# First loads in a new order, and stick-breaking steps set between projections

## The chip, the core and the metric

One NeuronCore of a Trainium2 chip runs the whole program. The metric is the device time of one launch in microseconds, lower is better. TensorE (PE) does matmuls, VectorE (DVE) and ScalarE (ACT) the elementwise work, GpSimd (POOL) and SyncE (SP) here mostly issue DMAs. Each engine runs its own instruction queue in order, and the engines meet only through semaphores.

## What is computed

Four transformer-like layers over 512 tokens of width 1024, in float32. Two parts of it matter here. Every layer begins with an RMS norm whose output is scaled and shifted by a modulation computed from a condition vector:

```
cond = silu(c)
mod  = cond @ ada_w[layer] + ada_b[layer]            # 6 x 1024 values
h    = rms_norm(x, mix_norm[layer]) * (1 + sc1) + sh1
```

Layer 0 then projects h to several outputs. The first, iq and ik, get rotary embeddings (tables of cosines and sines made from the positions) and feed a top-k choice of keys. The queries and keys of its attention, dq and dk, get another pair of tables.

Layer 1 has a pooling branch and stick-breaking attention with four heads of width 128:

```
u, sq, sk, sv = split(h @ w_in)                      # 512 columns each
o_pool = scale * ((trailing mean of u over 2, 4, 8, 16 tokens) - u) @ pool_w
q, k   = rms_norm(sq), rms_norm(sk)                  # per head
z      = q k^T / sqrt(128)
log_1m = where(s < t, log_sigmoid(-z), 0)
after  = reverse cumulative sum of log_1m over keys, less log_1m
w      = where(s < t, exp(log_sigmoid(z) + after), 0)
y      = concat(o_pool, w v) @ w_out
```

## The kernel before

Activations lie with features on partitions: a tile is 128 features x 512 tokens. `T(i)` is scratch tile i, `X(k)` the residual stream, `H(k)` the normed input. Weights come in chunks of 512 KB through a ring of four slots that SP fills, each when the slot's last use is over. Two PSUM rings of four banks each hold results: `proj` for projections, `mix` for everything else. The order in which banks are taken is written out in `mixing_keys` and `projection_keys`, and a bank is taken again only when its earlier user has emptied it. There is no planner: the order on each engine is the order of the program text.

Most projections are split: ScalarE rounds a weight chunk to a short float (`round_chunk`, `weight_hi`), VectorE computes the rest (`rest_chunk`, `weight_lo`), each in a ring of two, and TensorE does three matmuls per 128 rows: hi x hi, hi x lo, lo x hi. A feature tile of such a projection (`split_feature_tile`, L778) is 24 matmuls of 128x512; so is one of the four quarters of a token projection (`split_token_tiles`, L792). `first_pair` does tiles 0 and 1 of the first projection behind a norm together.

**The start.** ScalarE issues the loads of the sixteen modulation rows that the first norm needs (L1388), 512 KB each, four rows per semaphore. SP loads two tables of constants (`others`, `vectors`), the square matrices (`squares`, 768 KB) and x (2 MB), waits for the first eight rows, and then loads weights. GpSimd loads c, positions and small weights, waits for the last four rows and reloads the ring for the next modulation rows. ScalarE then computes silu(c). VectorE multiplies and reduces each row (L2002); before rows 4 and 8 it makes two rotation tables each (`rotation_table`, L1851 to L1855), whose sines ScalarE takes. ScalarE squares x for norm(0) behind the sines. VectorE sums six of the eight squares behind the sixteen rows (`sum_up`), TensorE sums over partitions (`row_sums`, L839), ScalarE takes the root, VectorE the reciprocal (L1899), TensorE spreads it (`spread_rows`, L848), VectorE scales the tiles (L1910) and ScalarE shifts them. The first projection (iq, L702) begins with the first shifted tile. Behind tile t of iq, TensorE does the swap of tile t-1 (L853) for its rotation, which needs a square matrix and ScalarE's copy of the projection.

**The stick-breaking stage.** The order is norm(2), cu (the pooled u), sq, sk, sv, then the pooling maps, then the heads. For sq and sk ScalarE copies and squares a tile (`head_stat`), TensorE sums it (L1008), ScalarE takes a root, VectorE a reciprocal and the product; the split of the next weight chunk stands between these in both queues. Then head h goes through: scores (TensorE, L1020, four banks), copies, exp and ln (ScalarE, `z_ready`), softplus and masks (VectorE, `sp_ready`), sums over keys (TensorE, L1027 and L1029), subtraction (VectorE), exp of the weights (ScalarE, `w_ready`), product with V (TensorE, L1041), rounding and rest for the output projection cdo. The loop over h overlaps neighbouring heads: scores of h, sums of h-1, product with V of h-2. `pair_step` then does tiles 0 and 1 of cdo for one of its eight inputs, and the other six tiles follow (L756).

Of the kernel before, what the change touches and what calls it, by code (L numbers as in the profile page):

```python
# [21 lines left out]
I32 = mybir.dt.int32  # L22
# [22 lines left out]
SPLIT_RING = 2  # L45
FIRST_ROWS = (0, 2, 4, 6, 8, 14, 16, 18, 20, 22, 24, 26, 28, 34, 36, 38)
# [100 lines left out]
for _name, _n in VECTORS:  # L147
# [10 lines left out]
    ("cu", "feat", 4, 8), ("sq", "feat", 4, 8), ("sk", "feat", 4, 8), ("sv", "tok", 4, 8), ("cdo", "loop", 8, 8),  # L158
# [14 lines left out]
SPLIT = ("abo", "up0", "dn0", "cu", "sq", "sk", "sv", "cdo", "up1", "dn1", "mqk", "mv", "mo", "mout", "up2", "dn2", "cout", "up3", "dn3", "rk", "rq", "rv", "fv", "ru", "rg", "br", "ro", "upr", "dnr")  # L173
# [38 lines left out]
def mixing_keys():  # L212
# [43 lines left out]
    return k  # L256

# [27 lines left out]
class Chip:  # L285


    def __init__(self, nc, ctx, dram):
# [37 lines left out]
        with ExitStack() as mlstm:  # L326
# [15 lines left out]
        self.first_rows = [sem(f"first_rows{i}") for i in range(4)]  # L342
        self.ada_landed = [sem(f"ada_landed{i}") for i in range(ADA_RING)]
        self.sem = {n: sem(n) for n in (
            "x_loaded", "c_loaded", "constants", "setup", "late", "pool_loaded", "dft_loaded", "cond_loaded", "ctx_loaded", "late_tables", "act_chain", "dve_chain",
# [65 lines left out]
    def cdo_hi(self, k):  # L411
        return self.R(k if k < 4 else 14 + k)

# [136 lines left out]
def sync_program(nc, sp, c):  # L550

    d, s = c.dram, c.sem
    for dst, src in ((c.other, d["others"]), (c.vec, d["vectors"]), (c.sq_const, d["squares"])):
        sp.dma_start(dst[:, :], src).then_inc(s["constants"], 16)
    sp.dma_start(c.x[:, :].rearrange("p (k t) -> p k t", k=KD), d["x"].rearrange("(k p) t -> p k t", p=P)).then_inc(s["x_loaded"], 16)

    proj = c.proj
    sp.wait_ge(c.first_rows[1], 16 * 4)
# [4 lines left out]
    for stage in STAGES:  # L563
# [59 lines left out]
def gpsimd_program(nc, pool, c):  # L623
# [23 lines left out]
    pool.wait_ge(c.first_rows[3], 16 * 4)  # L647
# [34 lines left out]
def tensor_program(nc, pe, c):  # L682
# [142 lines left out]
    def norm(r):  # L825

        n = stat_count(r)
        pe.wait_ge(s["sq_summed"], 6 * (n + 1))
        row_sums(r, T(SQ0), False)
        pe.wait_ge(s["sq_ready"], 8 * (n + 1))  # L830
        row_sums(r, T(SQ0 + KD - 1), True)
        pe.wait_ge(s["rstd_ready"], r + 1)
        spread_rows(r, 1)

    def row_sums(r, squares, last_half):

        bank = (mix.bank(("ss", r)) if last_half else open_bank(mix, ("ss", r)))[0:4, 0:P]
        for j in range(NB):
            last = mm(bank, c.const("pick")[:, 4 * j:4 * j + 4], squares[:, j * P:(j + 1) * P], start=not last_half and j == 0,  # L839
                      stop=last_half and j == NB - 1)  # L840
        if last_half:
            last.then_inc(mix.full_sem, 1)
# [19 lines left out]
    pe.wait_ge(s["constants"], 16 * 3)  # L862
    pe.wait_ge(s["setup"], 16 * 4)
    norm(0)
    for t in range(6):
# [5 lines left out]
        if t == 4:  # L871
            for n in range(NB):
# [126 lines left out]
    norm(2)  # L999
    first_pair("cu", 2, c.H_lo)  # L1000
    for t in range(2, 4):
        split_feature_tile("cu", t, c.H_hi, c.H_lo)
    for t in range(9):
        if t < 8:
            split_feature_tile("sq" if t < 4 else "sk", t % 4, c.H_hi, c.H_lo)
        if t >= 1:
            pe.wait_ge(*proj.emptied(("sq" if t <= 4 else "sk", (t - 1) % 4)))
            mm(open_bank(mix, ("stat_s", t - 1)), c.square("ones"), T(20 + (t - 1) % 2), start=True, stop=True).then_inc(mix.full_sem, 1)  # L1008
    split_token_tiles("sv", 0, c.H_hi, c.H_lo)
    for g in range(4):  # L1010
# [4 lines left out]
    pe.wait_ge(s["head_normed"], 8 + 4 + 8)  # L1015
    pe.wait_ge(*proj.emptied(("sv", 3)))
    for h in range(6):
        if h < 4:
            for j in range(NB):
                mm(open_bank(mix, ("z", h, j))[:, 0:S - P * j], T(14 + h)[:, j * P:(j + 1) * P], T(10 + h)[:, j * P:S],  # L1020
                   start=True, stop=True).then_inc(mix.full_sem, 1)
        if 1 <= h <= 4:
            pe.wait_ge(s["sp_ready"], h)
            sp = T(34 + 3 * ((h - 1) % 2), 3)
            for j in range(NB):
                bank = open_bank(mix, ("cum", h - 1, j))
                last = mm(bank[:, 0:S - P * j], c.square("later"), sp[:, TRI[j]:TRI[j + 1]], start=True, stop=j == NB - 1, skip_group_check=True)  # L1027
                for i in range(j + 1, NB):
                    last = mm(bank[:, P * (i - j):S - P * j], c.square("ones"), sp[:, TRI[i]:TRI[i + 1]], start=False,  # L1029
                              stop=i == NB - 1, skip_group_check=True)  # L1030
                last.then_inc(mix.full_sem, 1)
        if h == 5:
            for k in range(6):
                pe.wait_ge(*mix.emptied(("pool", k) if k < 4 else ("sb", k - 4)))
# [1738 lines left out]
```

## Time and profile before

| what | value |
|---|---|
| median of 3 runs | 3664.53 us (3664.01 to 3669.24) |
| the profiled execution | 3674.72 us |
| its span | 3673.1 us |
| busy: PE, PEld, DVE, ACT, POOL | 92%, 68%, 56%, 32%, 3% |
| mean granted TensorE clock | 0.957 of 2.4 GHz |

Busy time counts instructions that work, not waits. PEld are TensorE's weight loads, which overlap its matmuls. A clock of 1.00 is 2.4 GHz, 0.5 is 1.2 GHz. In a timeline, "[7.93 <-DVE scratch L1847]" means that the engine had been idle for 7.93 us and was released by that instruction. Nearly all VectorE tensor_tensor operations have the line of a helper, L1847, and ScalarE's have L1276.

### The profile page before, as it was taken

The numbers are of one execution on the slowest core, as the hardware profiler recorded it, in microseconds if no ns is written. First come the engines' busy times: TensorE is split into PE (matmuls) and PEld (weight loads), VectorE is DVE, ScalarE is ACT, GpSimd is POOL, SyncE is SP. The second block draws the span as 40 slices with busy tenths as digits, with TensorE's granted clock in tenths as the row PEclk, the third lists the DMA queues.
The fourth block names the chain that finished last, engine by engine and source line by source line (L and its number), as shares of the span: only waits on it lengthen the run. The fifth ranks groups of instructions, "written<-read, shape, count | busy, mean of one in ns | idle before, by whom it ended". The sixth has DMA issues, their size and how long they took to land. (4 is left out here: it accounts for less than half of the span.)

```text
span 3673.1 us, 37941 instructions
## 1 busy us (share of the span) xinstructions
PE 3367.4 (92%) x13358; PEld 2494.2 (68%) x13358; DVE 2059.4 (56%) x2808; ACT 1173.0 (32%) x1503; POOL 111.0 (3%) x204
## 2 busy tenths in 40 slices
PE   2998689999979999998999999799999999979997
PEld 1444468887647888666788864478887657758886
DVE  5757456544647884546666359766634553345523
ACT  2211333323443221444445210244423242232221
POOL 0000000000000000000000030000000000000000
PEclk9998699999989999999999999899999999989999
DMA  5332035643204563212223321123333222222232
GB/s 201 121 123 91 12 97 189 194 134 119 67 29 137 189 196 101 81 52 64 80 92 97 98 62 52 40 80 97 96 95 121 73 69 75 92 63 92 95 99 69
DMA packets 100417, 361.01 MB, mean 98 GB/s; under 512 B 11152, under 2 KB 11168, under 8 KB 100064
## 3 DMA queue, kind: packets, MB, share of 16 engines
q1 hardware_dynamic: 77936, 276.08, 23.9%
q0 software_dynamic: 20080, 75.27, 6.4%
q10 hardware_dynamic: 2304, 8.39, 0.6%
q8 instruction: 58, 0.95, 0.1%
q14 instruction: 39, 0.32, 0.0%
HBM read 357.59 MB, written 2.10 MB: 98 GB/s over the span
## 5 line engine op out<-in xcount | busy, mean ns | idle before, releaser
L1847 DVE TENSOR_TENSOR weight_lo<-weight_ring,weight_hi 128x1024 fp32r<-128x1024 f32 (+1 forms) x462 | 557.3, 1207 | 988.8 <-ACT weight_hi L1276 982.9
L1276 ACT ACTIVATE weight_hi<-weight_ring 128x1024 fp32r<-128x1024 f32 (+1 forms) x462 | 482.3, 1045 | 1515.0 <-PE proj_banks L756 1066.5
L756 PE MATMUL proj_banks<-h_lo,weight_hi 128*128 128x512 f32 x1776 | 694.5, 391 | 0.0
L756 PE MATMUL proj_banks<-h_hi,weight_hi 128*128 128x512 f32 x1344 | 525.7, 391 | 13.7 <-DVE weight_lo L1847 13.7
L756 PE MATMUL proj_banks<-h_hi,weight_lo 128*128 128x512 f32 x1344 | 525.8, 391 | 0.0
L756 PEld LDWEIGHTS proj_banks<-h_lo,weight_hi 128*128 128x128 f32 x1776 | 335.7, 189 | 70.1
L756 PEld LDWEIGHTS proj_banks<-h_hi,weight_hi 128*128 128x128 f32 x1344 | 254.0, 189 | 68.1 <-issue 15.3
L756 PE MATMUL proj_banks<-mid_lo,weight_hi 128*128 128x512 f32 x768 | 299.2, 390 | 0.0
L756 PEld LDWEIGHTS proj_banks<-h_hi,weight_lo 128*128 128x128 f32 x1344 | 253.5, 189 | 52.9
L756 PE MATMUL proj_banks<-mid_hi,weight_hi 128*128 128x512 f32 x704 | 273.9, 389 | 0.0
L756 PE MATMUL proj_banks<-mid_hi,weight_lo 128*128 128x512 f32 x704 | 273.9, 389 | 0.0
L702 PE MATMUL proj_banks<-h_tiles,weight_ring 128*128 128x512 f32 x592 | 260.9, 599 | 1.8 <-ACT h_tiles L1276 1.8
L1276 ACT ACT_TABLE_LOAD x133 | 170.6, 1283 | 259.0 <-PE proj_banks L756 109.8
L702 PEld LDWEIGHTS proj_banks<-h_tiles,weight_ring 128*128 128x128 f32 x592 | 113.5, 192 | 145.2 <-issue 143.2
L756 PE MATMUL proj_banks<-relu_hi,weight_hi 128*128 128x512 f32 x468 | 183.0, 391 | 7.6 <-DVE weight_lo L1847 7.6
L1847 DVE TENSOR_TENSOR scratch<-scratch 128x512 f32<-128x512 f32 (+5 forms) x226 | 160.1, 708 | 45.2 <-ACT small L1276 32.0
L1276 ACT ACTIVATE scratch<-proj_banks 128x512 f32<-128x512 f32 (+1 forms) x186 | 104.9, 574 | 229.9 <-PE proj_banks L702 127.5
L1855 DVE SCALAR_TENSOR_TENSOR scratch<-proj_banks,vectors,scratch 128x511 f32<-128x511 f32 (+3 forms) x208 | 155.2, 746 | 27.9 <-ACT scratch L1276 14.4
L756 PEld LDWEIGHTS proj_banks<-mid_lo,weight_hi 128*128 128x128 f32 x768 | 144.1, 188 | 30.2 <-issue 0.2
L1855 DVE SCALAR_TENSOR_TENSOR scratch<-scratch,vectors 128x512 f32<-128x512 f32 x212 | 159.4, 752 | 7.5
L756 PE MATMUL proj_banks<-relu_hi,weight_lo 128*128 128x512 f32 x404 | 157.8, 390 | 0.0
L756 PEld LDWEIGHTS proj_banks<-mid_hi,weight_hi 128*128 128x128 f32 x704 | 132.1, 188 | 27.5
(342 smaller groups left out, 4871.5 us busy)
## 6 DMA issues: line engine op xcount, KB each, us to landing
weight_ring<-in_w_up SPq DMA_DIRECT2D x176, 512.0 KB, 3.6
ada_ring<-in_ada POOLq DMA_DIRECT2D x96, 512.0 KB, 3.9
weight_ring<-in_w_dn SPq DMA_DIRECT2D x64, 512.0 KB, 3.5
weight_ring<-in_w_br SPq DMA_DIRECT2D x32, 512.0 KB, 3.6
weight_ring<-in_w_upr SPq DMA_DIRECT2D x32, 512.0 KB, 3.5
weight_ring<-in_w_dnr SPq DMA_DIRECT2D x32, 512.0 KB, 3.5
scratch<-in_ada POOLq DMA_DIRECT2D x24, 512.0 KB, 4.4
weight_ring<-in_w_dn SPq DMA_DIRECT2D x32, 384.0 KB, 3.1
```

The source lines that it names most:

```text
L702: last = mm(bank[:, 0:n], c.slot(chunk)[:, i * P:(i + 1) * P], rhs(k), start=k == 0, stop=k == sum(per) - 1)
L756: last = mm(proj.banks[:, u % RING, :], stationary(split0 + n)[:, w], moving(k), start=k + m == 0, stop=k == kt - 1 and m == 2)
L1276: return nc.scalar.activation(out, in_, func, **kw)
L1847: return v.tensor_tensor(out, a, b, op)
L1855: return v.scalar_tensor_tensor(out=out, in0=a, scalar=x, in1=b, op0=op0, op1=op1)
```

## The change

At the start: the row loads are shared, eight on ScalarE's queue and eight on SP's behind x; each row has its own semaphore. SP's wait for rows is gone; `squares` is loaded behind the second weight chunk. The rotation tables leave the row loop: the pair for i comes behind norm(0), the pair for q behind the top-k. norm(0) has no sums on VectorE: TensorE sums each squared tile as it comes, and the reciprocal is done before the last two rows. TensorE waits for `squares` before the first projection.

In layer 1: cu moves behind sv. Nine slots follow the four quarters of sv and the four tiles of cu, and slot numbers say what stands in each: scores, sums, product with V, pooling maps. `cdo_lo` gets tiles of its own and the weights of odd heads another place in scratch.

```diff
+ACT_ROWS = 8
+TRIG = (12, 13, 10, 11)
-    k += [("stat_s", t) for t in range(8)] + [("pool", g) for g in range(4)]
-    for h in range(6):
-        k += [("z", h, j) for j in range(NB)] if h < 4 else []
-        k += [("cum", h - 1, j) for j in range(NB)] if 1 <= h <= 4 else []
-        k += [("sb", h - 2)] if h >= 2 else []
+    k += [("stat_s", t) for t in range(8)] + [("z", 0, j) for j in range(NB)]
+    for slot in range(SB_SLOTS):
+        k += [("z", SB_SCORES[slot], j) for j in range(NB)] if slot in SB_SCORES else []
+        k += [("cum", SB_SUMS[slot], j) for j in range(NB)] if slot in SB_SUMS else []
+        k += [("sb", SB_VALUES[slot])] if slot in SB_VALUES else []
+        k += [("pool", g) for g in SB_POOLS.get(slot, ())]
+    k += [("sb", 3)]
+SB_SLOTS = 9
+SB_SCORES = {1: 1, 3: 2, 5: 3}
+SB_SUMS = {1: 0, 3: 1, 5: 2, 7: 3}
+SB_VALUES = {4: 0, 5: 1, 7: 2}
+SB_POOLS = {6: (0,), 7: (1,), 8: (2, 3)}
@@ sync_program
-    for dst, src in ((c.other, d["others"]), (c.vec, d["vectors"]), (c.sq_const, d["squares"])):
+    for dst, src in ((c.other, d["others"]), (c.vec, d["vectors"])):
+    for r in range(ACT_ROWS, len(FIRST_ROWS)):
+        sp.dma_start(c.T(FIRST_ROWS[r], 2), d["ada"][r]).then_inc(c.first_rows[r], 16)
-    sp.wait_ge(c.first_rows[1], 16 * 4)
+            if first + n == 1:
+                sp.dma_start(c.sq_const[:, :], d["squares"]).then_inc(s["squares_in"], 16)
@@ gpsimd_program
-    pool.wait_ge(c.first_rows[3], 16 * 4)
+    pool.wait_ge(c.first_rows[ACT_ROWS - 1], 16)
+    pool.wait_ge(c.first_rows[-1], 16)
@@ tensor_program
+        if r == 0:
+            for k in range(KD):
+                pe.wait_ge(s["sq_ready"], k + 1)
+                row_sums(r, T(SQ0 + k), k == 0, k == KD - 1)
...
     norm(0)
+    pe.wait_ge(s["squares_in"], 16)
...
+    norm(2)
+    first_pair("sq", 2, c.H_lo)
+    for t in range(1, 9):
+        if 2 <= t < 8:
+            split_feature_tile("sq" if t < 4 else "sk", t % 4, c.H_hi, c.H_lo)
+        pe.wait_ge(*proj.emptied(("sq" if t <= 4 else "sk", (t - 1) % 4)))
+        mm(open_bank(mix, ("stat_s", t - 1)), ...)
+    stick_scores(0)
+    split_token_tiles("sv", 0, c.H_hi, c.H_lo, between=stick_between)
+    for t in range(4):
+        split_feature_tile("cu", t, c.H_hi, c.H_lo)
+        stick_between(4 + t)
+    stick_between(8)
+    for k in (0, 1, 4, 5):
...
+        pair_step("cdo", k, c.cdo_hi, c.cdo_lo)
+    stick_values(3)
+    for k in (2, 3, 6, 7):
...
+        pair_step("cdo", k, c.cdo_hi, c.cdo_lo)
@@ scalar_program
-    for r, at in enumerate(FIRST_ROWS):
-        act.dma_start(T(at, 2), c.dram["ada"][r]).then_inc(c.first_rows[r // 4], 16)
+    for r in range(ACT_ROWS):
+        act.dma_start(T(FIRST_ROWS[r], 2), c.dram["ada"][r]).then_inc(c.first_rows[r], 16)
...
+    norm(0)
+    for n in range(2):
+        trig(n)
...
+    softplus_parts(0)
+    for slot in range(SB_SLOTS):
+        if slot < 8:
+            round_s(8 + slot + SPLIT_RING)
+        if slot == 3:
+            for t in range(4):
+                copy_out(proj, ("sv", t), T(24 + t))
+        if 4 <= slot < 8:
+            copy_out(proj, ("cu", slot - 4), T(slot - 4))
+        if slot in SB_SCORES:
+            softplus_parts(SB_SCORES[slot])
+        if slot in SB_SUMS:
+            stick_weights(SB_SUMS[slot])
+        if slot in SB_VALUES:
+            stick_hi(SB_VALUES[slot])
+        for g in SB_POOLS.get(slot, ()):
...
+    stick_hi(3)
@@ vector_program
     for r, at in enumerate(FIRST_ROWS):
-        dve.wait_ge(c.first_rows[r // 4], 16 * 4)
-        if r in (4, 8):
...
+        if r == len(FIRST_ROWS) - 2:
+            inverse_root(0)
+        dve.wait_ge(c.first_rows[r], 16)
...
     norm(0)
+    for n in range(2):
+        rotation_table(n)
+    dve.wait_ge(s["trig_ready"], 2)
...
+    softplus(0)
+    for slot in range(SB_SLOTS):
+        if slot < 8:
+            rest_s(8 + slot + SPLIT_RING)
+        if slot in SB_SCORES:
+            softplus(SB_SCORES[slot])
+        if slot in SB_SUMS:
+            stick_left(SB_SUMS[slot])
+        if slot in SB_VALUES:
+            sb_rest(SB_VALUES[slot])
+        for g in SB_POOLS.get(slot, ()):
+            pool_rest(g)
+        if 4 <= slot < 8:
+            pooled(slot - 4)
```

`stick_scores`, `stick_sums`, `stick_values`, `pool_map`, `softplus_parts`, `stick_weights`, `softplus`, `stick_left` hold the bodies of the old loop over h. The second pair of tables is made behind the top-k on VectorE; ScalarE takes its sines between its copies of gk and gv.

## Rows read from the trace of the kernel before

**Rows 1.** TensorE waits, whole run: group, releaser, us in total, times, longest
```profile
PE mix_banks L839 <- DVE scratch L1847: 88.5, 3, 64.4
...
PE mix_banks L1041 <- DVE scratch L1847: 16.1, 3, 7.9
```

**Rows 2.** Stretches: length, busy us of PE/PEld/DVE/ACT/POOL, PEclk, DMA share, GB/s
```profile
889.90:1121.70 231.80, 192.95 (x744) 143.11 (x744) 127.66 (x162) 97.21 (x133) 0.00 (x0) 0.91 0.17 52
...
1000.00:1073.00 73.00, 43.49 (x137) 26.78 (x136) 35.08 (x64) 43.32 (x60) 0.00 (x0) 0.79 0.04 11
...
1046.89:1053.60 6.71, 6.71 (x30) 4.58 (x28) 0.69 (x1) 6.16 (x12) 0.00 (x0) 1.00 0.01 2
...
921.53:926.57 5.04, 5.04 (x24) 4.18 (x23) 4.69 (x12) 1.91 (x3) 0.00 (x0) 1.00 0.32 104
...
155.00:332.00 177.00, 177.00 (x409) 78.28 (x410) 123.68 (x221) 37.83 (x60) 6.33 (x12) 0.99 0.32 104
```

**Rows 3.** The same view of ten microseconds near the start
```profile
30.00:40.00 10.00, 0.00 (x0) 0.00 (x0) 9.52 (x18) 1.26 (x2) 0.00 (x0) 1.00 1.03 410
```

**Rows 4.** DMA issues in the first 10 us: tile, queue, count, size, us to landing
```profile
x_tiles<-in_x SPq DMA_DIRECT2D x1, 2048.0 KB, 27.4
...
cond<-in_c POOLq DMA_DIRECT2D x1, 512.0 KB, 9.3
```

**Rows 5.** Timeline, start: start us, length, engine, line, tiles, count, idle
```profile
20.12 1.28 ACT L1276 ACT_TABLE_LOAD   x1 [20.12 <-issue]
...
22.50 1.22 DVE L2002 CUSTOM_DVE_ANT_0 scratch<-scratch,cond 128x1024 f32<-128x1024 f32 x1 [22.50 <-ACT cond L1276]
...
27.57 0.43 DVE L1999 CAST scratch<-scratch 128x512 f32<-128x512 int32 x1
...
36.13 1.23 DVE L2002 CUSTOM_DVE_ANT_0 scratch<-scratch,cond 128x1024 f32<-128x1024 f32 x1
...
42.57 1.62 POOL L640 DMA_DIRECT2D ada_ring<-in_ada  x3 [38.41 <-DMA scratch<-in_ada]
...
50.03 4.60 ACT L1276 ACTIVATE scratch<-x_tiles 128x512 f32<-128x512 f32 x7
...
59.85 4.33 DVE L1847 TENSOR_TENSOR scratch<-scratch 128x512 f32<-128x512 f32 x6
...
68.56 0.94 DVE L1899 RECIPROCAL scratch<-scratch 4x128 f32<-4x128 f32 x1 [4.38 <-ACT scratch L1276]
...
71.75 6.23 DVE L1855 SCALAR_TENSOR_TENSOR h_tiles<-x_tiles,gain,mix_banks 128x512 f32<-128x512 f32 x8 [2.25 <-PE mix_banks L848]
...
73.46 15.66 PE L702 MATMUL proj_banks<-h_tiles,weight_ring 128*128 128x512 f32 x32 [1.83 <-ACT h_tiles L1276]
...
88.96 1.02 PE L853 MATMUL mix_banks<-scratch,squares 128*128 128x512 f32 x2
...
89.82 7.03 PE L702 MATMUL proj_banks<-h_tiles,weight_ring 128*128 128x512 f32 x16
```

**Rows 6.** Timeline of VectorE at the gate arithmetic
```profile
271.14 5.78 DVE L1847 TENSOR_TENSOR scratch<-scratch 128x512 f32<-128x512 f32 x8 [32.05 <-ACT small L1276]
```

**Rows 7.** Timeline of TensorE: sq and sk projections, stick-breaking, output projection
```profile
945.44 0.47 PE L778 MATMUL proj_banks<-h_hi,weight_hi 128*128 128x512 f32 x1 [0.46 <-DVE weight_lo L1847]
...
952.62 0.47 PE L778 MATMUL proj_banks<-h_hi,weight_hi 128*128 128x512 f32 x1 [0.60 <-DVE weight_lo L1847]
...
1043.08 3.97 PE L1041 MATMUL mix_banks<-scratch 128*128 128x512 f32 x8 [7.93 <-DVE scratch L1847]
...
1088.89 0.47 PE L756 MATMUL proj_banks<-relu_hi,weight_hi 128*128 128x512 f32 x1 [1.88 <-DVE weight_lo L1847]
```

**Rows 8.** Timelines of ScalarE and VectorE in the stick-breaking heads
```profile
1002.00 3.16 ACT L1276 ACTIVATE scratch<-mix_banks 128x512 f32<-128x512 f32 x8 [0.17 <-PE mix_banks L1020]
...
1010.52 1.49 DVE L1855 SCALAR_TENSOR_TENSOR scratch<-scratch 128x1280 f32<-128x1280 f32 x1 [7.84 <-ACT scratch L1276]
...
1024.63 2.05 DVE L1847 TENSOR_TENSOR scratch<-scratch,mix_banks 128x512 f32<-128x512 f32 x4
```

More of the change, by code:

```diff
@@ L1014, in tensor_program @@
         mm(open_bank(mix, ("pool", g)), c.pool_w[:, g * P:(g + 1) * P], T(6 + g), start=True, stop=True).then_inc(mix.full_sem, 1)
[L1015 to L1034, printed above, removed]
-                pair_step("cdo", k, c.cdo_hi, c.H_lo)
-        if h >= 2:
-            pe.wait_ge(s["w_ready"], h - 1)
-            w = T(40 + 3 * (h % 2), 3)
-            bank = open_bank(mix, ("sb", h - 2))
-            for j in range(NB):
-                last = mm(bank[:, P * j:S], T(24 + j)[:, (h - 2) * P:(h - 1) * P], w[:, TRI[j]:TRI[j + 1]], start=j == 0,
-                          stop=j == NB - 1, skip_group_check=True)
-            last.then_inc(mix.full_sem, 1)
@@ L1422, in scalar_program @@
         copy_out(proj, ("gk", t), T(28 + t))
+    for n in range(2, 4):
+        trig(n)
     for t in range(4):
@@ new lines, in softplus_parts @@
+    def softplus_parts(h):
+        z, l = T(28 + 3 * (h % 2), 3), T(34 + 3 * (h % 2), 3)
+        for j in range(NB):
+            act.wait_ge(*mix.filled(("z", h, j)))
+            bank = mix.bank(("z", h, j))[:, 0:S - P * j]
+            f(z[:, TRI[j]:TRI[j + 1]], bank, ACT.Copy, scale=P ** -0.5)
+            st.last(f(l[:, TRI[j]:TRI[j + 1]], bank, ACT.Abs, scale=P ** -0.5), mix.emptied(("z", h, j)))
+        l = l[:, 0:TRI[4]]
+        st.link(f(l, l, ACT.Exp, scale=-1.0))
+        st.done(f(l, l, ACT.Ln, bias=c.const("one")), s["z_ready"])
@@ L1890, in sum_up, with inverse_root @@
             st.done(tt(H(0), H(0), H(k), ALU.add), s["final_summed"])
+    def inverse_root(r):
+        dve.wait_ge(*mix.emptied(("ss", r)))
+        st.done(v.reciprocal(T(RSTD)[0:4, P:2 * P], T(RSTD)[0:4, 0:P]), s["rstd_ready"])
     def norm(r):
-        if r not in NORM_AFTER:
+        if r not in NORM_AFTER and r > 0:
             for k in range(1, KD - 1):
@@ L2042, in vector_program @@
         st.link(ts(T(16 + b)[:, 0:width], score, -2e38, ALU.is_gt, NEG, ALU.mult))
+    for n in range(2, 4):
+        rotation_table(n)
+    dve.wait_ge(s["trig_ready"], 4)
+    st.link(ts(T(11), T(11), c.const("sign_q"), ALU.mult))
     ada_rows(15, 8)
@@ L2233, in vector_program, with pool_rest @@
                 s["head_normed"])
-    for n in range(12 + SPLIT_RING, 16):
-        rest_s(n)
-    for g in range(4):
+    def pool_rest(g):
         dve.wait_ge(s["pool_hi"], g + 1)
-        st.last(stt(c.H_lo(g), mix.bank(("pool", g)), c.v("pool_scale", g), c.cdo_hi(g).bitcast(F32), ALU.mult, ALU.subtract), mix.emptied(("pool", g)))
+        st.last(stt(c.cdo_lo(g), mix.bank(("pool", g)), c.v("pool_scale", g), c.cdo_hi(g).bitcast(F32), ALU.mult, ALU.subtract), mix.emptied(("pool", g)))
     def sb_rest(h):
@@ new lines, in sb_rest, with softplus @@
+        st.last(tt(c.cdo_lo(4 + h), mix.bank(("sb", h)), c.cdo_hi(4 + h).bitcast(F32), ALU.subtract), mix.emptied(("sb", h)))
+    def softplus(h):
+        z, sp = T(28 + 3 * (h % 2), 3)[:, 0:TRI[4]], T(34 + 3 * (h % 2), 3)[:, 0:TRI[4]]
+        dve.wait_ge(s["z_ready"], h + 1)
+        st.link(stt(sp, z, 0.0, sp, ALU.max, ALU.add))
+        for j in range(NB - 1):
+            w = slice(TRI[j], TRI[j] + P)
+            st.link(tt(sp[:, w], sp[:, w], c.square("strict"), ALU.mult))
+        w = slice(TRI[3], TRI[3] + P)
+        st.done(tt(sp[:, w], sp[:, w], c.square("strict"), ALU.mult), s["sp_ready"])
+        st.link(tt(z, z, sp, ALU.subtract))
+        for j in range(NB):
+            w = slice(TRI[j], TRI[j] + P)
+            st.link(tt(z[:, w], z[:, w], c.square("strict_neg"), ALU.add))
@@ new lines, in stick_left @@
+    def stick_left(h):
+        z = T(28 + 3 * (h % 2), 3)
+        for j in range(NB):
+            key = ("cum", h, j)
+            dve.wait_ge(*mix.filled(key))
+            w = z[:, TRI[j]:TRI[j + 1]]
+            st.last(tt(w, w, mix.bank(key)[:, 0:S - P * j], ALU.subtract), mix.emptied(key))
+    softplus(0)
+    for slot in range(SB_SLOTS):
+        if slot < 8:
+            rest_s(8 + slot + SPLIT_RING)
+        if slot in SB_SCORES:
+            softplus(SB_SCORES[slot])
+        if slot in SB_SUMS:
+            stick_left(SB_SUMS[slot])
+        if slot in SB_VALUES:
+            sb_rest(SB_VALUES[slot])
+        for g in SB_POOLS.get(slot, ()):
+            pool_rest(g)
+        if 4 <= slot < 8:
+            pooled(slot - 4)
```

206 lines of the change are left out of this document (87 added, 119 removed).

## The prediction

> **What bounds the kernel now.** I read the shares by engine first: TensorE is busy 92% of the span, so time can only be won where TensorE waits or runs at its lower clock. The list of TensorE's waits then names the places. The longest by far is 64.4 us before the first row-sum matmul of norm(0), and the heads' product with V (L1041) waits 16.1 us in three times [rows 1]. These are the two places that the change touches.
>
> The start: VectorE begins when silu(c) is there, at 22.50, because ScalarE first issues all sixteen modulation rows and is free only at 20.12. Then it alternates between row reductions and rotation tables, sums the squares of x, and the first projection starts at 73.46 [rows 5]. The DMA engines are full then, at 410 GB/s [rows 3].
>
> The stick-breaking stage runs from 889.9 to 1121.7. Its middle, 1000 to 1073, has 43.49 us of TensorE in 73, at a granted clock of 0.79; the stage as a whole has 0.91 [rows 2]. In this stretch each head waits in turn for ScalarE (copies, exp, ln), VectorE (softplus, masks, subtraction) and ScalarE again (exp), with no projection left to fill the gaps. Between 155 and 332 TensorE is busy without a pause [rows 2], so a shift at the start passes through there undiminished.
>
> **The start, step by step.** Before the last modulation row lands, these must come: sixteen rows of 512 KB, x, the two constant tables, c, positions and small weights, 12.48 MB by their shapes. Before the change the squares (0.79 MB) and four weight chunks (2.10 MB) moved in the same time, 15.36 MB in all, and GpSimd, which waits for the last rows, went on at 42.57 [rows 5]. 2.88 MB at 410 GB/s [rows 3] are 7.0 us, so the last row lands at 35.5.
>
> VectorE reduces a row in 1.27 us (four of them from 22.50 to 27.57, [rows 5]), and a row takes 0.524 MB / 410 GB/s = 1.28 us to land. ScalarE issues eight rows instead of sixteen, which took it until 20.12: about 10. c landed at 1.4 + 9.3 = 10.7 [rows 4], a table load and silu take 2.4 more, so VectorE starts near 13 instead of 22.5. Fourteen rows at 1.27 are then done at 31, ahead of the loads, the tables being gone from the loop. (Had it started at 22.5, sixteen rows would end at 42.8.) The reciprocal of norm(0), 0.94 [rows 5], now stands before the last two rows and delays them by about 1.0: row 13 lands at 33.0 and is done at 34.2, the reciprocal at 35.2, the rows at 36.5 and 37.8. Bias and gain take 0.4, and from the first scaled tile to the first projection are 1.71 (71.75 to 73.46): 39.9. The six sums (4.33) and the chain from sums to spread root (64.4 to 71.75) have left this path. They are replaced by eight row sums on TensorE, which is idle then. x has to be there in time. It was issued at 2.3 and landed 27.4 later, at 29.7 [rows 4], behind the squares; their 0.79 MB at the full rate are 1.9 us, at a third of it 5.8, so it now lands between 24 and 27.8. Seven squares of x take 4.60 [rows 5], a table load 1.28, the eighth, the row sums and the root about 1.9: 32 to 35.6, against a turn of the reciprocal at 34.2. The late end costs 1.4 us, which the next wait covers.
>
> The change adds a wait: TensorE waits for the squares before the first projection, and they now stand behind two weight chunks on SP's queue. Unshared they land when 14.32 of the 15.36 MB are through, 42.57 - 1.04/0.41 = 40.0. GpSimd's four rows start when the last first row has landed; if they take half the rate from 35.5 on, 1.84 MB need 9.0 us: 44.5. I take the middle, 42.2. All of TensorE's program is queued behind that wait. But a late start is partly made good: from the first matmul to the first swap were 15.50 us (73.46 to 88.96), paced by the scaling of tiles at 6.23 for eight, and at full pace two projections take 2 x 6.87 = 13.7 (a tile's 7.03 less the overlap, [rows 5]). So the first swap is at 55.9 instead of 88.96: 33.0 us earlier. With squares at 40.0 it would be 33.5, at 44.5 30.8.
>
> Two tables (the i pair) now follow the scaling on VectorE: 44.5 + 8.6 (27.57 to 36.13, with the cast, [rows 5]) = 53.1, the sine 0.63 and the sign 0.5 make 54.2. ScalarE's copy of the first projection is queued behind these sines and TensorE's swap behind the copy; both are ready 1 to 2 us before 55.9. Without that cover each late microsecond would cost one. The q pair (8.1 and a sign of 0.5) comes after the top-k, where VectorE has 32.05 us of idle time waiting for ScalarE's exponentials [rows 6]: nothing, and 8.6 if that slack were gone. ScalarE's copies of gv stand behind these sines, and the copies' input is later than they. SP's waits on rows vanish; GpSimd's reload of rows starts earlier by the same shift. The head is worth 33.0.
>
> **The stick-breaking stage.** The stage now runs sq, sk, sv, cu, with pieces of the heads after chosen quarters of sv and tiles of cu. Matmul work does not change. The terms: a tile or quarter of a projection 5.47 (six output tiles in 1121.7 - 1088.89, [rows 2, 7]); scores and sums of one head 6.7 at full clock [rows 2]; product with V 2.1; ScalarE from scores to z_ready 8.5 (1002.00 to 1010.52); VectorE's softplus and masks 5.6, its subtraction 2.05 [rows 8]; exp of the weights with its table load 2.6; the widest pooling 5.0 (the stretch from 921.53 to 926.57, [rows 2]).
>
> The sq and sk tiles run at a period of 7.18 (945.44 to 952.62, [rows 7]) because VectorE's reciprocal and split stand between them. This stays. But it is six tiles after the first pair and not eight, the first pair being sq itself. So TensorE is through with statistics at 950.7. From there its work to the end of the paired output steps is 26.8 (scores, sums) + 21.9 (sv) + 21.9 (cu) + 8.3 (V) + 3.4 (pool) + 10.9 (eight pair steps) = 93.2.
>
> I wrote all three engines' queues down in their new order and worked them forward with these durations. Three gaps stay on TensorE:
> First, the sums of head 1. VectorE does softplus(1) from 973.4, then the subtraction of head 0, until 981.1. ScalarE waits for it, then exp, two weight roundings, four copies of sv, and only then the copies of the scores that free the banks: 989.4. TensorE was done with the scores at 983.9: 5.5 us.
> Second, the product with V of head 1. It needs the bank of head 2's first sum, which VectorE frees after z_ready(3) at 1018.1, softplus 5.6 and the first subtraction 0.7: 1024.5. TensorE was free at 1016.6: 7.9 us.
> Third, the pooling of group 3, which VectorE reaches last: 5.8 us.
> With two of 0.5 this is 20.2 us. Each large gap is followed by matmuls at the lower clock: the product with V after a 7.93 gap took 3.97 [rows 7] and not 2.1, so 2 us each, 6 together. 950.7 + 93.2 + 20.2 + 6.0 = 1070.1. The same hand run of the old order ends at 1085.3 where the trace has 1087.0 (1088.89 - 1.88, [rows 7]), so I add 1.7: 1071.8, 15.2 earlier. The 1.88 before the third output tile stays, as does the rest of the stage. Bounds of this term: if every slot costs a gap of the longest kind, there are five slots with sums or V in them, 5 x 7.9 = 40 instead of 20, and the gain is -5; if the gaps and their slow clock halve, 28.
>
> **Sum.** 33.0 + 15.2 = 48.2. The profiled execution took 3674.72 us (span 3673.1), so it would take 3626.5. The runs shown have a median of 3664.53, 10.2 below the profiled one; the same saving gives 3616.3.
>
> **The rivals.** Changes of less than 0.2% (7 us) can't be told from none here.
> (a) The forecast: 40 to 56 us saved, 3608 to 3624. Chance 0.70.
> (b) x comes last. VectorE's queue is in order and the reciprocal stands before rows 14 and 15. If x landed only with the last row at 35.5, its squares, the root (7.8) and the reciprocal (0.9) would end at 44.2, the two rows at 46.8, bias and scaling put the first matmul at 48.9 and the swap at 64.4: the head saves 24.6, all 39.8, 3624.7. For it speaks that x is the largest transfer and landed 27.4 us after its issue; against it, that more stood before it then [rows 4]. Chance 0.09. The Trainium skill (DMA: Bandwidth & Descriptors, queues, rings and completion order) says that a DMA engine takes turns between the queues packet by packet, so a queue with shorter packets gets fewer bytes; x's rows are half as long as a modulation row's. Its slow landing agrees.
> (c) The stage's gaps only move. The roundings of weights stand behind softplus in both queues, and if a projection also waits for its split in each of the five slots, the stage saves 0: 33 in all, 3631.5. For it: VectorE and ScalarE are in-order and nearly every slot has a handshake. Against: in the run by hand each split was ready before its tile. Chance 0.12.
> (d) Slower: TensorE stays at the lower clock. If after the first gap every further one came before the clock had recovered, all 99 us of work from 950.7 to the pair steps would run at half speed, 99 more, of which 20 fill the gaps: 79 lost against 48 saved, 3695. It turns slower from 68 of the 99 us at half speed. For it: 0.79 between 1000 and 1073. Against it: right behind the slow product with V the clock was 1.00, from 1046.89 to 1053.60 [rows 2], and the projections between make blocks of 5 us and more. The Trainium skill (TensorE: Matmul & The Clock Gate, loop structure matters more than you think) has the rule that long waits between bursts put the clock at half; the trace agrees with the row of 3.97. Chance 0.02.
> (e) The gaps are half as long as computed: 13 us more, 3603. Chance 0.07.
>
> **The numbers.** The likeliest is 3616.3, its own range 3608 to 3624. From 3604 to 3630 hold (a), (b) and about half of (c) and (e), 0.85 to 0.9 if each is right, and I leave the rest for errors of mine. Faster by over 0.2% are (a), (b), (c) and (e): 0.97, with 0.01 for no change and 0.02 for (d).
>
> **What would show it.** First projection matmul at 40 to 44, first swap near 56, GpSimd's first reload near 35.5: the head. If the matmul is later and its releaser is the DMA of the squares, the queue term was off; if VectorE idles before its reciprocal, it was x. VectorE's long idle at the gate arithmetic should be near 23 instead of 32. In the stage: waits of about 5 to 8 us before the sums of head 1, the product with V of head 1 and the pooling of group 3, and 216.6 us from the first pair to the end of the output projection. Waits of L778 or L792 on weight_lo between slots would speak for (c), a granted clock below 0.8 from there for (d). The prediction fails if the stage is no shorter or if the last row does not land before 40.

## The result, and the profile after

The changed kernel takes 3626.61 us (median; 3613.92 to 3628.97) against 3666.89 of the kernel before on the same chip: a ratio of 0.989, 95% interval 0.9873 to 0.9907, so 34 to 47 us faster. The forecast was 3616.3. A second measurement, on another occasion, gave 3621.46 against 3664.46: 0.9882 (0.9867 to 0.9897), 38 to 49 us. The saving forecast, 48.2, lies just past the upper end of the first and just inside that of the second. The median is 10.3 above the forecast: outside its likeliest range, 3608 to 3624, and inside the 3604 to 3630 that was given with it.

The profiled execution took 3627.46 (span 3625.8), where 3626.5 was forecast for it. That agreement flatters: two errors meet in it, as the experiments show.

Timelines of the changed kernel's start (start us, length, engine, line, operation, count, idle before it and what ended it), from all four engines, to be held against [rows 5]:
```profile
0.87 4.74 ACTq L1439 DMA_DIRECT2D scratch<-in_ada  x8
...
2.27 19.38 SPq L577 DMA_DIRECT2D scratch<-in_ada  x8
...
10.31 1.06 ACT L1327 ACTIVATE cond<-cond 128x1024 f32<-128x1024 f32 x1 [3.39 <-DMA cond<-in_c]
...
25.30 4.60 ACT L1327 ACTIVATE scratch<-x_tiles 128x512 f32<-128x512 f32 x7 [13.94 <-DMA x_tiles<-in_x]
...
26.03 8.93 PE L868 MATMUL mix_banks<-scratch,others 128*4 128x128 f32 x64 [26.03 <-ACT scratch L1327]
...
35.52 0.94 DVE L1963 RECIPROCAL scratch<-scratch 4x128 f32<-4x128 f32 x1 [1.29 <-ACT scratch L1327]
...
36.00 1.62 POOL L663 DMA_DIRECT2D ada_ring<-in_ada  x3 [31.83 <-DMA scratch<-in_ada]
...
39.44 6.23 DVE L1923 SCALAR_TENSOR_TENSOR h_tiles<-x_tiles,gain,mix_banks 128x512 f32<-128x512 f32 x8
...
41.15 1.19 PE L726 MATMUL proj_banks<-h_tiles,weight_ring 128*128 128x512 f32 x1 [3.48 <-ACT h_tiles L1327]
```
Silu no longer waits for ScalarE's queue but for c. GpSimd's reload, which waits for the last rows, comes at 36.00 (forecast 35.5), the scaling of the tiles at 39.44 instead of 71.75. The first projection is released by ScalarE's tile at 41.15, not by the DMA of the squares, whose load was issued at 23.7 and landed 16.1 later: the added wait costs nothing, and the 42.2 forecast for it was too late by 1.0. The first swap is at 57.76, against 88.96 and a forecast of 55.9.

TensorE's waits in the stick-breaking stage of the changed kernel, from 920 to 1050 (group, releaser, us in total, times, longest):
```profile
PE mix_banks L1056 <- DVE scratch L1915: 8.1, 2, 7.9
PE mix_banks L1042 <- ACT scratch L1327: 6.3, 2, 5.6
PE mix_banks L1065 <- DVE scratch L1915: 5.9, 1, 5.9
```
These are the three gaps that the prediction computed as 7.9 (product with V of head 1), 5.5 (sums of head 1) and 5.8 (pooling of group 3). The stage in the timeline of TensorE: its first pair, the first matmuls behind the three gaps, and the third output tile:
```profile
864.16 0.80 PE L740 MATMUL proj_banks<-h_hi,weight_hi 128*128 128x512 f32 x1 [1.65 <-ACT h_hi L1327]
...
964.03 2.05 PE L1042 MATMUL mix_banks<-scratch,squares 128*128 128x512 f32 x2 [5.60 <-ACT scratch L1327]
...
999.60 3.84 PE L1056 MATMUL mix_banks<-scratch 128*128 128x512 f32 x8 [7.85 <-DVE scratch L1915]
...
1029.32 2.07 PE L1065 MATMUL mix_banks<-scratch 128*128 128x512 f32 x2 [5.86 <-DVE scratch L1915]
...
1047.32 0.70 PE L780 MATMUL proj_banks<-relu_hi,weight_hi 128*128 128x512 f32 x2 [1.89 <-DVE weight_lo L1915]
```
The matmuls behind each gap run slowly, as forecast: 3.84 for the product with V that takes 2.39 elsewhere. The third output tile starts at 1047.32, 183.2 after the first pair. In the kernel before the first pair is at
```profile
890.15 0.79 PE L716 MATMUL proj_banks<-h_hi,weight_hi 128*128 128x512 f32 x1 [1.66 <-ACT h_hi L1276]
```
and the third output tile at 1088.89 [rows 7], 198.7 later. 15.6 saved, 15.2 forecast.

### The profile page after: what moved, and what is told of

It is laid out like the page before. It is cut to its first block and busy times, and to the rows that moved or that the text cites. A ratio compares the mean times of both kernels' runs of the same rounds, so it can differ in the third digit from the quotient of the medians.

```text
span 3625.8 us, 38035 instructions
## 1 busy us (share of the span) xinstructions
PE 3365.5 (93%) x13406; PEld 2495.2 (69%) x13406; DVE 2055.4 (57%) x2802; ACT 1174.1 (32%) x1504; POOL 111.0 (3%) x204
## 5 line engine op out<-in xcount | busy, mean ns | idle before, releaser
L780 PE MATMUL proj_banks<-h_lo,weight_hi 128*128 128x512 f32 x1728 | 676.2, 391 | 0.0
L780 PEld LDWEIGHTS proj_banks<-h_lo,weight_hi 128*128 128x128 f32 x1728 | 326.7, 189 | 67.8
L780 PE MATMUL proj_banks<-relu_hi,weight_hi 128*128 128x512 f32 x516 | 194.5, 392 | 7.6 <-DVE weight_lo L1915 7.6
L1915 DVE TENSOR_TENSOR scratch<-scratch 128x512 f32<-128x512 f32 (+6 forms) x220 | 155.9, 709 | 37.5 <-ACT small L1327 24.4
```

What stands on the lines that cost most here:

```text
L780: last = mm(proj.banks[:, u % RING, :], stationary(split0 + n)[:, w], moving(k), start=k + m == 0, stop=k == kt - 1 and m == 2)
L1915: return v.tensor_tensor(out, a, b, op)
```

## The experiments

Ratios are to the kernel before, run on the same chip. Times of single runs without a ratio are not compared; those runs were made for their profiles. Where a kernel has lines added, its line numbers are up to six higher than those of the changed kernel.

**The two halves.** *start_only* is the kernel before with the start of the change, *stage_only* with the new order of the stage; *after_again* is the changed kernel beside them. The edit of *stage_only*, cut to its core:
```diff
+SB_SCORES = {1: 1, 3: 2, 5: 3}
+SB_SUMS = {1: 0, 3: 1, 5: 2, 7: 3}
+SB_VALUES = {4: 0, 5: 1, 7: 2}
...
+    split_token_tiles("sv", 0, c.H_hi, c.H_lo, between=stick_between)
```
and of *start_only*:
```diff
+    for r in range(ACT_ROWS):
+        act.dma_start(T(FIRST_ROWS[r], 2), c.dram["ada"][r]).then_inc(c.first_rows[r], 16)
...
+        dve.wait_ge(c.first_rows[r], 16)
```


> The kernel before with the start of the change alone (rows, squares, tables, row sums); the stick-breaking stage is the old one. Theory A (the two parts are independent, each keeps what the traces show): first swap at 57.8 us, 31 earlier; of that 26 arrive at norm(1), and 26 to 31 at the end: timed ratio to before 0.992 to 0.993. Rival B (the shift is eaten later, by waits on weights or the reload of modulation rows, and the whole measured gain is the stage's): 0 to 15 us at the end, ratio 0.996 to 1.

> The kernel before with the new order of the stick-breaking stage alone; the start is the old one. Theory A: from the first pair of the stage to norm(3) 216 us instead of 231.6, and 15.2 to 15.6 us less at the end, ratio 0.9958. Rival B (the stage's gain shows up only because it starts at another phase of the granted clock): stage 225 or more, ratio 0.998 to 1.

> The changed kernel once more, beside its two halves on one chip. Theory A: the two halves add up, so the ratio is the product of theirs, 0.988 to 0.989, 41 to 46 us. Rival B (they overlap or disturb each other): less than the larger half plus 5 us.

Measured: *start_only* 3637.0, ratio 0.9923 (0.9909 to 0.9936), 23 to 33 us faster. *stage_only* 3654.68, ratio 0.9973 (0.9963 to 0.9983), 6 to 14 us faster. Their product is 0.9896, inside *after_again*'s interval. So both parts are real, and within these intervals nothing speaks against their adding up; some three quarters of the gain is the start. But *stage_only*'s own profile shows the full 15.6 in the stage, and its median gains 9.8. That is below what the profile promised, and its interval ends at 13.6.

**The profile of before, once more.**

> The kernel before, unchanged, profiled once more. Theory A (the profile shown of before had more of the lower clock in stretches that the change does not touch): first swap at 88.9 to 89.0 again, norm(1) at 503 to 507 instead of 509.0, the stage from norm(2) to norm(3) 237 to 238.5, span near 3663. Rival B (that profile is the typical one and the kernels made since gain outside the changed code): norm(1) at 509, span 3670 or more.

Its first row sum of norm(1), in the timeline of TensorE:
```profile
506.90 1.04 PE L839 MATMUL mix_banks<-scratch,others 128*4 128x128 f32 x8
```
The profile shown of before has this at 509.02, and *stage_only*, whose start is the old one, at 503.54. The same instructions on the same waits differ by 5.5 us there; at the end the two profiles of before are 9.5 apart (3674.72 and 3665.21). Theory A holds in kind: the profile shown is one of the longer executions. The norm(1) of *before_again* is at the late end of the range I gave, its span is 3663.5.

**Where the spread comes from.** The whole stage, norm(2) to norm(3), in windows (length, busy us of PE, PEld, DVE, ACT, POOL, granted clock, DMA share, GB/s). In the changed kernel:
```profile
857.19:1080.17 222.98, 190.72 (x769) 142.47 (x768) 133.16 (x167) 99.58 (x136) 0.00 (x0) 0.94 0.18 57
```
and in *warm_start* (below), whose stage has the same instructions:
```profile
846.57:1074.49 227.92, 195.30 (x770) 145.72 (x769) 133.21 (x167) 99.63 (x136) 0.00 (x0) 0.92 0.18 56
```
TensorE's idle time is 32.3 and 32.6. What differs is its busy time, by 4.6, at a granted clock of 0.92 instead of 0.94: VectorE and ScalarE work for the same time to 0.1. The stage took 222.98, 223.00 and 222.96 in *after*, *after_again* and *stage_only*, and 227.92, 227.94, 227.89 and 227.77 in *warm_start*, *rows_on_act*, *bytes_in_front* and *tables_in_loop*. The Trainium skill (TensorE: Matmul & The Clock Gate, What's actually happening) says that how many matmuls run before the clock rises varies from run to run; the two windows agree, and show a price of 5 us a stage.

The old stage took 238.5 in the profile shown of before, 237.4 in *before_again* and 237.3 in *start_only*. Four of seven profiles have the long form, so the new order is worth 14.3 to 15.6 in one form and 9.3 to 10.8 in the other, and *stage_only*'s 9.8 lies where a mixture of both would. The runs without a profile can't be sorted into the two, so that is an inference. Nor is chance told from the chip: the three profiles from chip 1 are long, the two from chip 3 short.

Stretches that no edit touches vary too: from the row sums at 2736.38 to the end the changed kernel took 889.4, *before_again* 889.2 and *start_only* 882.2, with TensorE busy for 829.9, 829.9 and 822.8 of it, so the ends of two profiles can differ by 7 us without any change.

**Two causes named for the start.** *rows_on_act* lets ScalarE issue all rows; *bytes_in_front* moves loads ahead of SyncE's rows:
```diff
-ACT_ROWS = 8
+ACT_ROWS = 16
...
+    sp.wait_ge(c.first_rows[8], 16)
```
```diff
+    sp.dma_start(c.sq_const[:, :], d["squares"]).then_inc(s["squares_in"], 16)
+    for n in range(4):
+        sp.dma_start(c.slot(n), d["w_iq"][n]).then_inc(c.landed[n % RING], 16)
     for r in range(ACT_ROWS, len(FIRST_ROWS)):
...
```


> The changed kernel, but ScalarE issues all sixteen rows (SyncE's queue waits for row 8 before its weights). Theory A (silu, and with it VectorE's first row, waits until ScalarE has issued its rows): silu ends near 22.5, VectorE is busy without a pause until 43.9, first projection at 46 instead of 41.2, first swap near 62.2, 4.5 later. Rival B (the landing of the rows sets the pace, VectorE follows): first projection within 1 us of 41.2.

> The changed kernel, but SyncE issues the squares and the first four weight chunks (2.88 MB) ahead of its eight rows. Theory A (the start is bound by bytes before the last row): last row 7.0 us later, first projection near 46.4 instead of 41.2, GpSimd's reload near 43. Rival B (VectorE's 1.28 us a row sets the end, the loads have slack): first projection within 1.5 us of 41.2.

The first projection matmul of *rows_on_act*, in the timeline:
```profile
45.28 3.75 PE L727 MATMUL proj_banks<-h_tiles,weight_ring 128*128 128x512 f32 x4 [2.85 <-ACT h_tiles L1328]
```
and timelines of *bytes_in_front*: a row of VectorE, GpSimd's reload, the first projection:
```profile
33.71 1.23 DVE L2072 CUSTOM_DVE_ANT_0 scratch<-scratch,cond 128x1024 f32<-128x1024 f32 x1 [7.80 <-DMA scratch<-in_ada]
...
43.05 1.62 POOL L665 DMA_DIRECT2D ada_ring<-in_ada  x3 [38.89 <-DMA scratch<-in_ada]
...
47.02 1.19 PE L728 MATMUL proj_banks<-h_tiles,weight_ring 128*128 128x512 f32 x1 [2.56 <-ACT h_tiles L1329]
```
Both as theory A has it. With the rows on ScalarE the first projection is 4.1 later (46 expected, 45.28 seen) and the first swap, at 62.04, 4.3. The Trainium skill (DMA: Bandwidth & Descriptors, Issuing engines are not separate DMA queues) says that issuing from several engines saves only sequencer time, usually small beside the transfer. Here sixteen issues held ScalarE until 20.12 [rows 5] and eight for 4.74, and in this place it decides when silu can run. With 2.88 MB in front VectorE waits 7.80 for one row and the reload moves from 36.00 to 43.05: 7.05, as 2.88 MB at 410 GB/s say. The start has two constraints that are nearly even; either alone holds it. A third is the row sums, for which the reciprocal waited 1.29 in the changed kernel and not at all in these two. But norm(1) came at 483.4 and 481.8 in these two, and at 478.9 to 484.6 in the five profiles with the changed kernel's start (*after*, *after_again*, *spread*, *left_first*, *values_later*): 4 to 6 us at the first swap were not to be seen there (below).

**The tables.** All four go back between the rows:
```diff
+        if r in (4, 8):
...
+            for n in (r // 2 - 2, r // 2 - 1):
+                rotation_table(n)
```


> The changed kernel with all four rotation tables back between the modulation rows on VectorE, two before row 4 and two before row 8. Theory A (the tables lengthen VectorE's chain, which has only some 5 us of idle time among the rows): VectorE busy from 11.4 to about 50, first projection near 51.6 instead of 41.2, first swap near 67, 9 later. Rival B (the landing of the rows hides the tables): first projection before 44.5.

```profile
48.19 2.07 PE L877 MATMUL mix_banks<-scratch,others 4*128 4x128 f32 x8 [12.28 <-DVE scratch L1963]
...
52.83 16.86 PE L726 MATMUL proj_banks<-h_tiles,weight_ring 128*128 128x512 f32 x32 [2.56 <-ACT h_tiles L1327]
```
In these rows of its TensorE timeline the spread of the root waits 12.28 for the reciprocal, and the first projection is 11.7 later than with the tables behind the scaling; the swap, at 69.53, 11.8. I expected 10.4 and 9. Of the three pieces undone this is the largest. The sums and the root with its reciprocal, which held VectorE's path from 59.85 to 71.75 [rows 5] and now lie beside the rows, were not put back by themselves.

**The clock of the first projections.** TensorE gets matmuls to do while it would be idle; their result is overwritten unread.
```diff
+    for r in range(6):
+        pe.wait_ge(c.first_rows[r], 16)
+        for _ in range(2):
+            mm(proj.bank(("iq", 0)), c.other[:, 0:P], c.other[:, 0:S], start=True, stop=True)
     norm(0)
+    for _ in range(2):
+        mm(proj.bank(("iq", 0)), c.other[:, 0:P], c.other[:, 0:S], start=True, stop=True)
```


> The changed kernel with 14 more matmuls on TensorE that nobody reads: two behind each of the first six modulation rows, two between the spread root and the first projection. Theory A (the start lost 2 us against the forecast because idle TensorE is granted 1.2 GHz): the row sums end near 33 instead of 35.0, the reciprocal does not wait (1.29 gone), the first projections run at the full clock from the start, first swap at 54.4 instead of 57.8, set then by the copy behind the second sine; 3 us less at the end. Rival B (VectorE's scaling of the tiles paces the first projection and the sines the swap, whatever the clock): the swap at 57 or later, nothing at the end.

The windows from the first projection matmul to the first swap, first of the changed kernel, then of *warm_start*:
```profile
41.15:57.76 16.61, 16.61 (x33) 7.21 (x34) 12.88 (x22) 8.05 (x11) 0.00 (x0) 0.83 0.42 164
```
```profile
41.57:56.17 14.60, 13.97 (x32) 5.96 (x32) 12.89 (x22) 8.06 (x12) 0.00 (x0) 1.00 0.47 178
```
At the full clock the two projections take 13.97 instead of 16.61; the forecast had 13.7. The tiles are scaled as fast as before (6.23 for eight), so it was the clock that paced the projections, as theory A says; of rival B the sines remain. The swap is then 1.6 earlier, no longer 3.4, because the copy behind the second sine ends last (0.64 of idle): the cover of 1 to 2 us that the prediction named is used up.

The other half of theory A, the row sums, was not put to the test by this edit. Stretches of 3 us show it by the number of matmul records in them (the x behind TensorE's busy time), two of the changed kernel and one of *warm_start*:
```profile
26.03:29.03 3.00, 3.00 (x15) 1.85 (x16) 2.38 (x3) 2.87 (x5) 0.00 (x0) 1.00 1.02 406
31.03:34.03 3.00, 3.00 (x30) 2.39 (x28) 2.92 (x5) 1.00 (x3) 0.00 (x0) 1.00 1.04 414
```
```profile
26.59:29.59 3.00, 3.00 (x15) 1.80 (x16) 2.34 (x3) 2.87 (x5) 0.00 (x0) 0.50 1.03 410
```
In the changed kernel the first 3 us hold 15 row-sum records and a later 3 us hold 30: half pace, then full pace. Its clock column says 1.00 for both, but its trace has no clock record before 29.7, and the view then shows 1.00. *warm_start* has a record there, 0.50 with the same 15, after TensorE had been idle for 3.61 between the last unread matmul and the row sums. So both run their first row sums at 1.2 GHz, in 8.93 and 8.79 us for all 64 records, and the reciprocal still waits 1.10. At full pace the row sums would end near 33, just behind the last square (32.08), and the reciprocal would not wait; that is an estimate from these rows, and no run tried it.

The same holds for the kernel before at its first projection, where the count goes from 4 to 8:
```profile
73.46:76.46 3.00, 3.00 (x4) 1.44 (x5) 2.86 (x5) 2.75 (x5) 0.00 (x0) 1.00 0.00 0
78.46:81.46 3.00, 3.00 (x8) 1.33 (x7) 0.64 (x2) 0.28 (x1) 0.00 (x0) 1.00 0.00 0
```
Timed, *warm_start* is at 3614.0, ratio 0.9874 (0.9858 to 0.9891): not to be told from *after_again*.

**The three gaps.** Each was ascribed to a place in VectorE's order. *left_first* exchanges two steps, *values_later* moves one product, and *spread* does both and puts the pooling of group 3 behind the first four output pairs (of its edit the places are shown, not the helpers):
```diff
+        if slot in SB_SUMS:
+            stick_left(SB_SUMS[slot])
         if slot in SB_SCORES:
             softplus(SB_SCORES[slot])
-        if slot in SB_SUMS:
-            stick_left(SB_SUMS[slot])
```
```diff
-SB_VALUES = {4: 0, 5: 1, 7: 2}
+SB_VALUES = {4: 0, 6: 1, 7: 2}
```
```diff
-SB_POOLS = {6: (0,), 7: (1,), 8: (2, 3)}
+SB_POOLS = {6: (0,), 7: (1,), 8: (2,)}
...
+    pool_map(3)
     stick_values(3)
```


> The changed kernel with one exchange on VectorE: stick_left(h) before softplus(h+1). Theory A (hand run of the queues): the wait before the sums of head 1 falls from 5.6 to 2.4, the one before the product with V of head 1 from 7.85 to nothing, that before the pooling of group 3 stays at 6.0; the stage is 12.4 shorter, 210.6 from norm(2) to norm(3) against 223.0. Rival B (the exchange only passes the wait on to the later softplus): the sum of the three waits stays within 3 of 19.3.

> The changed kernel with the product with V of head 1 one slot later. Theory A: its wait falls from 7.85 to 2.5, the other two stay at 5.6 and 5.8; the stage is 5.5 shorter, 217.5. Rival B (the head behind it waits in its place): the sum of the waits stays within 2 of 19.3. A stage some 5 longer with the same waits, as in three runs so far, is the lower granted clock in it and counts for neither.

> The changed kernel with the three gaps taken on at their causes: on VectorE stick_left(h) stands before softplus(h+1); the product with V of head 1 one slot later; the pooling of group 3 behind the first four output pairs. The same hand run of the three queues that gave gaps of 5.5, 7.9 and 5.8 now gives 2.4, 0 and 0.6 (each cause is the in-order queue of VectorE), and no slow clock behind them: the stage ends 19.9 us earlier, 196 us from first pair to norm(3). Rival (the gaps move into the next handshake, since VectorE has as much to do as before): 5 us or less.

TensorE's waits in the stage, 920 to 1050, with *left_first*:
```profile
PE mix_banks L1065 <- DVE scratch L1915: 5.9, 1, 5.9
PE mix_banks L1042 <- ACT scratch L1327: 3.3, 2, 2.6
...
PE mix_banks L1056 <- DVE scratch L1915: 0.8, 1, 0.8
```
with *values_later*:
```profile
PE mix_banks L1042 <- ACT scratch L1327: 6.3, 2, 5.6
PE mix_banks L1065 <- DVE scratch L1915: 5.9, 1, 5.9
PE mix_banks L1056 <- DVE scratch L1915: 3.4, 3, 2.4
```
and with *spread*:
```profile
PE mix_banks L1042 <- ACT scratch L1328: 3.3, 2, 2.6
...
PE mix_banks L1056 <- DVE scratch L1921: 0.8, 1, 0.8
PE mix_banks L1065 <- DVE scratch L1921: 0.4, 1, 0.4
```
Every one of the three waits changed as the hand run said, and those that were left alone stayed; a new one of 0.8 came, before the product with V of head 2: expected 2.4 / 0 / 6.0, 5.6 / 2.5 / 5.8 and 2.4 / 0 / 0.6. The stage took 213.2 (210.6 expected), 216.8 (217.5) and, in this window of *spread*, 203.2 against 223.0:
```profile
856.47:1059.63 203.16, 186.70 (x770) 140.65 (x769) 133.40 (x167) 99.76 (x136) 0.00 (x0) 0.97 0.19 63
```
Of those 19.8 (19.9 expected), 15.8 are idle time and 4.0 busy time at a higher granted clock. In *left_first* the waits fell as expected and the busy time did not (191.19 against 190.72): the 2 us of slow clock that should have gone with the gap stayed. *spread* is the fastest version: 3602.69, ratio 0.9826 (0.9813 to 0.984), some 19 less than the changed kernel beside it.

**Both together.**

> The new orders of run spread and the unread matmuls of run warm_start together. Theory A (independent): spread's time less what the warm start gives; first projections at the full clock, the swap at 56.2, stage 203 from norm(2) to norm(3): 3598 to 3602, ratio 0.982. Rival B (the warm start's gain was the phase of the clock in that run): the same as spread, 3603, or more.

3604.11, ratio 0.9832 (0.9815 to 0.985). It can't be told from *spread*, nor theory A's 3598 to 3602 from rival B's 3603, so the warm start isn't shown to be worth anything at the end. Its profiled execution had a mean granted clock of 0.914 and took 3629; the five others had 0.959 to 0.964 and took 3596 to 3608. The stage there, 203.7 long, is as expected.

## Why the prediction was right, and by how much it was off

**The start, mechanism right but for the clock, term too large.** 33.0 forecast, 28 timed (23 to 33). The last row (35.5 against 36.00), the tiles and the order of events came as worked out. Four things did not.

First, "paced by the scaling of tiles ... at full pace two projections take 13.7": the 15.50 of the kernel before were a slow clock at their start (4 matmuls in 3 us, then 8), and the new start has a slow clock there too. The two projections took 16.61 at a granted clock of 0.83, and *warm_start* shows that the clock was the reason. This is the step that failed, and it cost 2.9.

Second, the row sums. The root was put 7.8 behind the first square; it ended at 35.42, 10.1 behind 25.30, because the 64 records of row sums took 8.93, the first of them at half pace. x had landed early in its range, so the reciprocal's wait came out at 1.29, inside the 1.4 allowed, by luck. In the other profiles with this start it was 1.42 (*start_only*) to 2.30 (*spread*). It made the first projection 1.2 later than the 39.9 of this chain.

Third, the squares were to hold the first projection until 42.2 and had landed before 41.15. That it came only 1.0 off its forecast is this error against the one before it. The swap came 31.2 earlier, where 33.0 was forecast.

Fourth, "a shift at the start passes through there undiminished" [rows 2]. From first swap to norm(1) the three kernels with the old start took 420.1, 417.4 and 415.0 us; six with the new one (*start_only*, *after*, *after_again*, *spread*, *left_first*, *values_later*) 421.5 to 425.5. By the means, 417.5 and 423.8, some 6 of the 31 are given back on the way. Up to 2.2 of it is a new wait of TensorE, for the weights of dv:
```profile
211.07 14.43 PE L835 MATMUL proj_banks<-weight_ring,h_tiles 128*128 128x512 f32 x33 [1.70 <-DMA weight_ring<-in_w_dv]
```
In this row of the changed kernel it is 1.70; four of those six have it (1.66 to 2.16), and the kernels with the old start have none. In the DMA issues around it (count, size, median us to landing) these loads land 8.8 us after their issue in the changed kernel,
```profile
weight_ring<-in_w_dv SPq DMA_DIRECT2D x4, 512.0 KB, 8.8
```
and 4.0 in the kernel before:
```profile
weight_ring<-in_w_dv SPq DMA_DIRECT2D x4, 512.0 KB, 4.0
```
What shares the DMA engines with them there was not tried. The rest is no wait but slower matmuls: on this way TensorE was busy for 358.9 to 364.0 us with the old start and for 365.4 to 368.0 in these six. It shows best from the first swap to the indexer's scores (first matmul of 64x256), where TensorE is idle for 2.3 in all of them: 44.8, 44.9 and 46.5 with the old start, 46.5 three times and 48.1 three times with the new one, at granted clocks of 0.92, 0.89 and 0.86. Whether the new start makes the lower clock more frequent or three and six profiles drew it by chance stays open: *bytes_in_front* and *warm_start* took 418.4 and 417.1 from swap to norm(1), which is also why the 5.7 us later swap of the one and the 1.6 us earlier swap of the other are not what their norm(1) shows; *rows_on_act* and *tables_in_loop* took 421.4 and 422.3.

**The stage, mechanism right, gaps right to 0.1.** Forecast 15.2, in the profiles 14.3 to 15.6 or 9.3 to 10.8, timed 9.8 (6.2 to 13.6). The step that fell short is "2 us slow clock after each" gap: in the long form the stage loses 4.6 more, also behind waits under 2 us. The rows [rows 7] from which I took 2 us were one draw from one execution.

**The reference point.** The profile of before was 8 to 10 us longer than the median runs, mostly in stretches that the change does not touch. Its difference to the profile of after, 47.3, so looks like the 48.2 forecast, and the timed difference, 40 to 43, doesn't.

**The rivals.** (a) holds in its terms; its 3608 to 3624 was missed by 2.6 with the first median and met with the second, 3621.46. (b) is out: x landed before 25.3, and the reciprocal waited for row sums. It gives 3624.7, near the measured time, by a mechanism that isn't there. (c) is out by the stage alone. (d) has a true core: a lower clock took back some 5 us in the stage, not 79. (e) is out: the gaps have their full length. The top-k slack, VectorE's idle time ahead of the gate arithmetic, went from 32.05 [rows 6] to 24.4, the last figure in this group of the page of after (busy us and mean ns ahead of it, then idle); "near 23" was the forecast.
```profile
L1915 DVE TENSOR_TENSOR scratch<-scratch 128x512 f32<-128x512 f32 (+6 forms) x220 | 155.9, 709 | 37.5 <-ACT small L1327 24.4
```

## What to carry to other kernels

Queues written out by hand and worked forward with measured durations gave each of the three handshake gaps to 0.2 us here, and also the edits that removed them; a gap's cause is often what stands before the releasing instruction in its own queue. A gain argued for idle time survives in the timed median, what goes with the clock varies by several us from run to run: take the reference from more than one profile. At the start of a trace, count the matmuls in a stretch before believing a clock of 1.00. At a start, look for everything that stands in front of the first needed result in each queue (issues, tables, bytes); the constraints were nearly even, and undoing any one of three moved the first swap back by 4 to 12 us.

## What was not expected of the hardware

- A queue of sixteen 512 KB loads held ScalarE for 19.23 us, one of eight for 4.74. The number is not all: in the changed kernel SyncE's eight, issued behind x and beside ScalarE's, held its queue for 19.38. In the timeline of the kernel before:
```profile
0.86 19.23 ACTq L1388 DMA_DIRECT2D scratch<-in_ada  x16
```
- Before the first clock record of a trace the view says 1.00 while TensorE runs at half pace: 15 records of row sums in 3 us there, 30 in 3 us later (changed kernel, norm(0)).
- The same stage with the same waits takes 223.0 or 227.9 us, and repeats each of the two to 0.2 us.
